# Decoder layer on one core: the output projection's second half with split attention operands, a 64 + 64 column tile for the sample rows, and gate-up low parts one slot ahead

## What is computed

```python
def mix_out(o_attn, conv_y, attn_out_g, conv_out_g, w_o):
    a = rmsnorm(o_attn.reshape(b, t, D_ATTN), attn_out_g)
    v = rmsnorm(conv_y, conv_out_g)
    return jnp.concatenate([a, v], axis=-1) @ w_o          # (576 x 1024) @ (1024 x 1024)
xp = xp + g1 * mix_out(...)                                # residual, per token set
h  = rmsnorm(xp, ln2_g) * (1 + sc2) + sh2
xp = xp + g2 * ((silu(h @ w_gate) * (h @ w_up)) @ w_down)  # w_gu: 1024 x 5632, w_down: 2816 x 1024
```

## Time and profile before

| | us |
|---|---|
| median of 3 runs | 933.33 |
| profiled execution | 940.86 |
| its span in the trace | 939.1 |
| TensorE busy | 910.1 (97%) |
| VectorE busy | 637.4 (68%) |
| ScalarE busy | 413.6 (44%) |
| GpSimd busy | 281.0 (30%) |

### The profile page before, as it was taken

How to read it: one execution, slowest core, us unless ns; L and a number is a source line. 1 busy time by engine, 2 the same in 40 slices (tenths; PEclk the granted TensorE clock), 3 DMA queues, 4 the chain that set the end, 5 groups by cost and what they waited for, 6 DMA issues and landing times.

```text
span 939.1 us, 16499 instructions
## 1 busy us (share of the span) xinstructions
PE 910.1 (97%) x6285; PEld 769.7 (82%) x6285; DVE 637.4 (68%) x1251; ACT 413.6 (44%) x823; POOL 281.0 (30%) x277
## 2 busy tenths in 40 slices
PE   6999999999999999999999998999999999999998
PEld 5777888899996666866775498999999999888886
DVE  3546585488837676768472799899889898443544
ACT  3655562142135343666840574444444446333221
POOL 4110100000015442444600217776777774000000
PEclk9989999999999999999999999999999999999999
DMA  8998603235248987196103163333333333522201
GB/s 266 386 362 272 199 27 114 90 119 222 89 139 309 335 322 266 57 303 173 36 1 112 68 180 85 96 90 91 91 95 103 108 101 109 194 90 90 73 0 51
DMA packets 84188, 138.83 MB, mean 148 GB/s; under 512 B 4180, under 2 KB 54948, under 8 KB 79759
## 3 DMA queue, kind: packets, MB, share of 16 engines
q1 hardware_dynamic: 74578, 96.26, 32.1%
q0 software_dynamic: 9248, 41.39, 12.5%
q10 hardware_dynamic: 284, 0.13, 0.1%
HBM read 130.58 MB, written 11.31 MB: 151 GB/s over the span
## 4 chain that ended last, share of the span: by engine, by line
PE 86%; DVE 6%; DMA 4%; ACT 2%; issue 2%; POOL 1%; SPq 0%; DVEq 0%; ACTq 0%
PE bank L2389 18%; PE bank L2391 18%; PE bank L2390 18%; PE bank L2383 9%; PE bank L2469 3%; PE bank L2910 3%; DMA wring<-in_w_ada 2%; PE bank L2750 2%; PE bank L2418 2%; PE bank L2720 2%; PE bank L2929 2%; PE bank L2883 2%; PE bank L2398 2%; PE bank L2399 2%; PE bank L2674 1%
## 5 line engine op out<-in xcount | busy, mean ns | idle before, releaser
L2389 PE MATMUL bank<-s,ring_hi 128*128 128x288 f32 x620 | 184.6, 298 | 2.7 <-DVE ring_lo L528 2.7
L2390 PE MATMUL bank<-s,ring_lo 128*128 128x288 f32 x620 | 183.6, 296 | 0.0
L2391 PE MATMUL bank<-s,ring_hi 128*128 128x288 f32 x620 | 183.0, 295 | 0.0
L2389 PEld LDWEIGHTS bank<-s,ring_hi 128*128 128x128 f32 x620 | 116.8, 188 | 3.2 <-DVE ring_lo L528 3.1
L2391 PEld LDWEIGHTS bank<-s,ring_hi 128*128 128x128 f32 x620 | 117.4, 189 | 0.0
L2390 PEld LDWEIGHTS bank<-s,ring_lo 128*128 128x128 f32 x620 | 117.1, 189 | 0.0
L528 DVE TENSOR_TENSOR ring_lo<-mem,ring_hi 128x512 fp32r<-128x512 f32 x84 | 108.3, 1325 | 0.8 <-POOL mem L980 0.5
L2383 PEld LDWEIGHTS bank<-cst,arena 128*128 128x128 f32 (+1 forms) x538 | 62.3, 148 | 21.0 <-issue 12.3
L2383 PE MATMUL bank<-cst,arena 128*128 128x128 f32 (+1 forms) x538 | 72.1, 288 | 7.5 <-DMA arena<-in_cache_k_cmp,idx 6.6
L528 DVE TENSOR_TENSOR dn_w<-wring,dn_w 128x2048 fp32r<-128x2048 f32 (+1 forms) x11 | 23.1, 2096 | 65.9 <-ACT dn_w L525 65.9
L900 POOL DMA_INDIRECT arena<-in_cache_k_slc,idh x16 | 15.4, 963 | 172.9 <-PE bank L2391 167.3
(11 more groups left out here) (385 smaller groups left out, 2112.9 us busy)
## 6 DMA issues: line engine op xcount, KB each, us to landing
wring<-in_w_gu SPq DMA_DIRECT2D x44, 512.0 KB, 5.3
wring<-in_w_ada SPq DMA_DIRECT2D x16, 1024.0 KB, 11.0
wring<-in_w_in SPq DMA_DIRECT2D x10, 1024.0 KB, 5.1
wring<-in_w_down SPq DMA_DIRECT2D x10, 1024.0 KB, 5.0
wring<-in_w_ada SPq DMA_DIRECT2D x16, 512.0 KB, 5.8
proj<-in_x_prompt SPq DMA_DIRECT2D x4, 512.0 KB, 11.9
mem<-in_state_k_win POOLq DMA_DIRECT2D x8, 256.0 KB
mem<-in_state_v_win POOLq DMA_DIRECT2D x8, 256.0 KB
```

What stands on the lines that cost most here:

```text
L2389: pe.matmul(dst, sh, ml, start=first and k == 0, stop=False)
L2390: pe.matmul(dst, sl, mh, start=False, stop=False)
L2391: ins = pe.matmul(dst, sh, mh, start=False, stop=last and k == len(pairs) - 1)
```

## The change

1. The heads of half n = 1 become split products, as in half n = 0. The third weight block (`wo`, 1, 0) gets high parts `last_hi` (four 512-column casts by ScalarE) and low parts `last_lo` (four subtractions by VectorE, in place of the raw block in the weight ring). `o_hi` and `o_lo` have to live through half n = 1, and move from `hbuf` to four places for the high part and onto `oT` itself for the low part; the casts and subtractions that made them in one instruction are now four, one for each slice.
2. The sample tile of half n = 0 (t = 4) goes through `products_tail`: the operands of convolution and heads carry 64 high and 64 low columns. ScalarE copies the lower half of the bank to `otmp`, VectorE adds it, and the gate multiplication follows as an instruction of its own.
3. One of the new places of `o_hi` is where the high part of operand m = 7, segment 0, lives later, so ScalarE makes that part later: it moves from behind m = 5 to behind `first_copy(1)`.
4. VectorE does `slot_rest(14)` ahead of its loop and `slot_rest(p + 8)` in each step, that in a step with m = 3 ahead of L2341 and L2344 as before.

```diff
-SEG_HIGH = [(0, 4), (0, 8), (0, 5), (0, 7), (0, 6), (1, 4), (1, 8), (2, 8), (2, 4), (1, 5), ...
+SEG_HIGH = [(0, 4), (0, 8), (0, 5), (0, 6), (1, 4), (1, 8), (2, 8), (2, 4), (0, 7), (1, 5), ...
...
+        o_hi = [pairs_at(f"o_hi{k}", z, c0, WIDE)[:, :] for k, (z, c0) in enumerate(((arows, 0), (arows, WIDE), (mem, 4 * TOK), (mem, 8192)))]
+        o_lo = pairs_at("o_lo", uvT, 0, 4 * TOK)[:, :].rearrange("p (k n) -> p k n", k=4)
+        last_hi = [pairs_at(f"wo_last{k}", z, c0, 512)[:, :] for k, (z, c0) in
+                   enumerate(((proj, 4608), (proj, 5120), (selb, 0), (mem, 8192 + WIDE)))]
...
ScalarE
+            def outputs_high(c0, c1):
+                for k in range(4):
+                    ins = high(act.copy, o_hi[k][:, c0:c1], oT[:, k, c0:c1])
+                ins.then_inc(o_high, 1)
...
-            high(act.copy, o_hi[:, :, 0:384], oT[:, :, 0:384]).then_inc(o_high, 1)
+            act.wait_ge(gates_out, 16)
+            outputs_high(0, 384)
...
-            high(act.copy, o_hi[:, :, 384:TOK], oT[:, :, 384:TOK]).then_inc(o_high, 1)
+            outputs_high(384, TOK)
+            weights(act, ("wo", 1, 0))
+            for k in range(4):
+                ins = high(act.copy, last_hi[k], last_raw[:, k])
+            ins.then_inc(wo_high, 1)
...
+            want_filled(act, ("wo", 0, 4))
+            act.copy(otmp[0:TS, :], ps(("wo", 0, 4))[TS:2 * TS, :]).then_inc(wo_tail, 1)
...
-                    for m in (5, 7, 6):
+                    for m in (5, 6):
                         sums_high(0, m)
...
             first_copy(1)
+            sums_high(0, 7)
...
VectorE
+            def outputs_low(c0, c1):
+                for k in range(4):
+                    if c1 == TOK:
+                        low(dve, o_hi[k][:, TOK:WIDE], oT[:, k, SEQ:TOK], o_hi[k][:, SEQ:TOK]).then_inc(dve_step, 1)
+                        steps[0] += 1
+                        dve.wait_ge(dve_step, steps[0])
+                    ins = low(dve, o_lo[:, k, c0:c1], oT[:, k, c0:c1], o_hi[k][:, c0:c1])
+                ins.then_inc(o_low, 1)
...
-            low(dve, c_lo, vT[:, :, 256:TOK], c_hi).then_inc(c_low, 1)
+            low(dve, c_lo, vT[:, :, 256:SEQ], c_hi[:, :, 0:256])
+            low(dve, c_hi[:, :, 320:384], vT[:, :, SEQ:TOK], c_hi[:, :, 256:320]).then_inc(c_low, 1)
...
+                        if not n and t == 4:
+                            dve.wait_ge(wo_tail, 1)
+                            frees(dve.tensor_tensor(x1t[0:P, :], ps(key)[0:P, :], otmp[0:P, :], ALU.add), key)
+                            want_emptied(dve, key)
+                            link(dve.tensor_tensor(x1t[0:P, :], x1t[0:P, :], gbc[0:P, t // 4, cols], ALU.mult))
...
+                    if not n and t == 2:
+                        dve.wait_ge(wo_high, 3)
+                        for k in range(4):
+                            ins = low(dve, last_lo[:, k], last_raw[:, k], last_hi[k])
+                        ins.then_inc(wo_low, 1)
...
             slot_rest(13)
+            slot_rest(14)
...
-                if p == 7 or FAST[p - 1][1] != 3:
-                    slot_rest(p + 7)
+                slot_rest(p + 8)
...
                 if m == 3:
-                    if p + 1 < NFAST:
-                        slot_rest(p + 8)
...
TensorE, project_conv
+                    if t == 4:
+                        products_tail(ps(key)[:, :], [(c_hi[:, kk, 256:384], (wo_hi[1][:, kk], wo_lo[1][:, kk])) for kk in range(4)],
+                                      True, False)
+                        return
...
TensorE, project_heads
+                pe.wait_ge(wo_low, 3 if n else 1)
+                pe.wait_ge(o_low, 1 + t // 3)
+                w = [(last_hi[k], last_lo[:, k]) if n else (wo_hi[0][:, k], wo_lo[0][:, k]) for k in range(4)]
+                if not n and t == 4:
+                    fills(products_tail(ps(key)[:, :], [(o_hi[k][:, SEQ:WIDE], w[k]) for k in range(4)], False, True), key)
                     return
-                wt = weights(pe, ("wo", n, 0))
-                for kk in range(4):
-                    last = pe.matmul(ps(key)[0:TM[t], :], oT[:, kk, 128 * t:128 * t + TM[t]], wt[:, kk, :], start=False, stop=kk == 3)
-                fills(last, key)
+                fills(products(ps(key)[0:TM[t], :], [((o_hi[k][:, c], o_lo[:, k, c]), w[k]) for k in range(4)], False, True), key)
```

More of the change, by code:

```diff
@@ L74 @@
 SEGS = ((2, 0, 96), (3, 96, 224), (4, 224, 288))
-SEG_HIGH = [(0, 4), (0, 8), (0, 5), (0, 7), (0, 6), (1, 4), (1, 8), (2, 8), (2, 4), (1, 5), (1, 7), (2, 5), (1, 6), (2, 7), (2, 6),
+SEG_HIGH = [(0, 4), (0, 8), (0, 5), (0, 6), (1, 4), (1, 8), (2, 8), (2, 4), (0, 7), (1, 5), (1, 7), (2, 5), (1, 6), (2, 7), (2, 6),
             (0, 3), (1, 3), (2, 3)]
@@ L432, in decoder_kernel @@
         wo_lo = [pairs_at(f"wo_lo{x}", wring, 2048 * r, 2048)[:, :].rearrange("p (k n) -> p k n", k=4) for x, r in enumerate(wo_at)]
-        c_hi, c_lo = (pairs_at(f"c_pair{y}", proj, 1280 * y, 1280)[:, :].rearrange("p (k n) -> p k n", k=4) for y in range(2))
-        o_hi, o_lo = (pairs_at(f"o_pair{y}", hbuf, 4 * TOK * y, 4 * TOK)[:, :].rearrange("p (k n) -> p k n", k=4) for y in range(2))
+        c_hi, c_lo = (pairs_at(f"c_pair{y}", proj, 1536 * y, 4 * n)[:, :].rearrange("p (k n) -> p k n", k=4) for y, n in enumerate((384, 256)))
+        o_hi = [pairs_at(f"o_hi{k}", z, c0, WIDE)[:, :] for k, (z, c0) in enumerate(((arows, 0), (arows, WIDE), (mem, 4 * TOK), (mem, 8192)))]
+        o_lo = pairs_at("o_lo", uvT, 0, 4 * TOK)[:, :].rearrange("p (k n) -> p k n", k=4)
+        last_hi = [pairs_at(f"wo_last{k}", z, c0, 512)[:, :] for k, (z, c0) in
+                   enumerate(((proj, 4608), (proj, 5120), (selb, 0), (mem, 8192 + WIDE)))]
+        last_raw = wch[:, chunk_of["wo", 1, 0] % WR]
+        last_lo = pairs_at("wo_last_lo", wring, 2048 * (chunk_of["wo", 1, 0] % WR), 2048)[:, :].rearrange("p (k n) -> p k n", k=4)
         g_rows = nc.dram_tensor("g_rows", [128, 512], F32).ap()
@@ L1322, in _ @@
             act.wait_ge(kvc_stored, 32)
-            high(act.copy, c_hi, vT[:, :, 256:TOK]).then_inc(c_high, 1)
+            high(act.copy, c_hi[:, :, 0:320], vT[:, :, 256:TOK]).then_inc(c_high, 1)
             weights(act, ("wo", 0, 1))
@@ L2095, in _ @@
             dve.wait_ge(o_high, 1)
-            low(dve, o_lo[:, :, 0:384], oT[:, :, 0:384], o_hi[:, :, 0:384]).then_inc(o_low, 1)
+            outputs_low(0, 384)
             key = ("oT", 4)
@@ L2112, in _ @@
             dve.wait_ge(o_high, 2)
-            low(dve, o_lo[:, :, 384:TOK], oT[:, :, 384:TOK], o_hi[:, :, 384:TOK]).then_inc(o_low, 1)
+            outputs_low(384, TOK)
             def second_norm(t):
@@ L2915, in project_heads @@
                 key = ("wo", n, t)
-                if n == 0:
-                    c = slice(128 * t, 128 * t + TM[t])
-                    pe.wait_ge(wo_low, 1)
-                    pe.wait_ge(o_low, 1 + t // 3)
-                    fills(products(ps(key)[0:TM[t], :], [((o_hi[:, kk, c], o_lo[:, kk, c]), (wo_hi[0][:, kk], wo_lo[0][:, kk]))
-                                                         for kk in range(4)], False, True), key)
-                    return
-                if t < 4:
-                    pe.wait_ge(o_ready, 1 + t // 3)
-                else:
-                    want_emptied(pe, ("oT", 4))
-                wt = weights(pe, ("wo", n, 0))
-                for kk in range(4):
-                    last = pe.matmul(ps(key)[0:TM[t], :], oT[:, kk, 128 * t:128 * t + TM[t]], wt[:, kk, :], start=False, stop=kk == 3)
-                fills(last, key)
+                c = slice(128 * t, 128 * t + TM[t])
+                pe.wait_ge(wo_low, 3 if n else 1)
[3 more added lines that the diff above has]
+                    fills(products_tail(ps(key)[:, :], [(o_hi[k][:, SEQ:WIDE], w[k]) for k in range(4)], False, True), key)
+                    return
+                fills(products(ps(key)[0:TM[t], :], [((o_hi[k][:, c], o_lo[:, k, c]), w[k]) for k in range(4)], False, True), key)
             def turn_sample():
```

10 lines of the change are left out of this document (5 added, 5 removed).

## The result

| | before | after |
|---|---|---|
| median (4 runs each) | 933.93 us (933.22 to 936.35) | 946.13 us (944.69 to 947.50) |
| ratio, 95% interval | | 1.0136 [1.0116, 1.0155] |
| profiled execution, its span | 940.86, 939.1 us | 945.81, 944.0 us |

A forecast was written before the change was run, and what follows sets the result against it. TensorE was taken to bound the kernel. The terms -1.9 (sample tile), -2.84 (heads) and +0.2 (order of low parts) sum to -4.5 us, so 928.8 us for the median, range 924.5 to 931.2.

The forecast's parts named there:

- What bounds the kernel: TensorE, busy 97% of the span; the output projection is bound by TensorE alone, with VectorE and ScalarE having time to spare.
- Parts 1 and 2: Output projection: split heads of half n = 1 give 2.84 us in tiles 0 to 3, 0.76 in tile 4; sample tile 1.9.
- The cover: Projection: low parts are ready before heads (0, 3), with 4.4 us to spare, and before (1, 0), so TensorE doesn't wait.
- What arrives: At the gate-up stage: 4.74 us of TensorE's 5.5 us arrive; 0.76 us becomes a wait at `turn_last`.
- The walk through the first tiles: Start of gate-up: VectorE and GpSimd turns followed to slot 19 in both orders; +0.2 us, bounds -1.2 and +1.2 us.
- the last sentence of part 4: Later gate-up stage: every slot has more than 1 us of margin in either order, so nothing is gained there.
- no wait from 600 on: Sign to look for: TensorE has no wait in the gate-up stage from 600 us on.
- The rival "slower": First tiles f: GpSimd takes each turn, VectorE loses 12 times 1.2 us over three tiles; 943 us, chance 0.03.
- The clock: Rival: behind slot 19's wait, now in pieces, the clock may not fall to 0.50; saves 1.7 us, 927.1 us, chance 0.22.

The follow-up runs named there:

- e1: Kernel after with VectorE's old order of slot low parts, projection edits kept; 929.74 us, ratio 0.9958 to before.
- e3: Kernel after with the low part of slot m = 3 moved behind the bank read L2355 in the m = 6 step; 930.13 us, ratio 0.9960 to before.
- e4: Kernel after with the low part in the m = 3 step moved behind the two gated products; 927.83 us, ratio 0.9944 to before.
- e6: The order of e3, with the two gated products of f = 1 moved to the end of step p = 12; 929.10 us, ratio 0.9956 to before.
- e10: e6 with the order of e4 for f > 1; 927.32 us, ratio 0.9939 to before.
- e9: Kernel after with a wait added: from f = 4 GpSimd makes slot m = 5 (L977) only behind the previous tile's gated products; 929.03 us, ratio 0.9957 to before.
- e8: Kernel after with TensorE doing product f = 8, m = 1 four more times, 6.4 us of additional work; 942.49 us, ratio 1.0089 to before.

## Why the prediction was wrong

The forecast was a gain of 4.5 us; it is a loss of 12.2 us. Point by point, in the order of its parts:

- **What bounds the kernel** was right for before. TensorE bound it, and it bounds e1, e3, e4, e6 and e10.
- **Parts 1 and 2 were right, but for 0.3 us.** The sample tile of half n = 0 gave 1.89 us where 1.9 was forecast. From the start of one tile of half n = 1 to the start of the next, tiles 0 to 2 gave 0.69 to 0.70 us each (0.71 was forecast), tile 3 gave 0.53, its distance holding the transposes of tile 2 (520.98, 0.09 us late, and 1.03 us long where they had taken 0.96), and tile 4 gave 0.68 (0.76 was forecast), its borders costing what was put at nothing. The cover held: no wait of TensorE at heads (0, 3) or (1, 0).
- **What arrives was right in its sum, its parts were a little off.** 4.79 us where 4.74 was forecast. TensorE came to the stage 5.19 us sooner (68.38 to 63.19) instead of 5.5, and 0.40 us of it went at `turn_last`, its wait being 0.34 and not 0.8 to 0.9. That the sum is right to 0.05 us is in part luck: two parts were off by 0.3 and by 0.4 us, and offset each other.
- **The walk through the first tiles was mis-sized.** The rows have 3.6 us of waits up to 600 us against 2.7, and by starts it is 4.9 against 3.2: 1.7 us more where the walk said +0.2, at most +1.2. It looked at slots 17 and 19 alone; there are five waits (565.52, 0.61 us, and 585.88, 588.31 among them).
- **The step that failed is the last sentence of part 4**, that later in the stage every slot has more than 1 us of margin in either order, and with it the sign "no wait from 600 on". The margins were read off the old order, slot by slot, against TensorE alone. But an in-order engine that waits 0.42 us for a cast delays what is queued behind it, here a bank read which GpSimd needs, behind which four GpSimd instructions stand, the last of which VectorE waits for. The prediction had asked this question of the waits that part 1 adds (what is queued behind it, and who waits for that) and not of the one that part 4 adds each tile. What the runs showed in its place is a ring of 12.25 us a tile against TensorE's 11.20, and sixteen waits, 16.6 us. The durations that the ring is made of, the 1.5 us of a lost turn among them, were to be had from the timelines of before; their chaining was not done.
- **The rival "slower" named half of the mechanism with the wrong reach.** The turns that the products lose are a needed link: with these gone the tile takes 11.36 us (e9). It gave them three tiles, and they last for 16; that its 943 us came near is luck, then. Its reason against, that the same instruction was back to 0.44 us from 587.54 on, described where the old order puts L972, not what the new order does to it; and it was read off L2341 alone, while the product behind it still lost its turn:

```profile
587.91 1.55 DVE L2344 TENSOR_TENSOR arena<-selb,uvT 128x288 f32<-128x288 f32 x1
```

  In before L972 starts at 653.18, 0.02 us behind the instruction that follows the two products (653.16), and it is 0.39 us behind L2344's start in every tile from 596.79 on. So they were neighbours in every tile, at a distance that a delay of the products by a few tenths eats up.
- **The other link**, the low part of slot m = 3 ahead of the read, was no rival at all. Cutting this link alone gives TensorE its 11.20 us a tile back (e3), as does taking the products out from behind the wait (e4); cutting the other leaves 0.16 us of the 1.04 (e9).
- **The clock.** It stayed at 1.00 through the gate-up stage of after: neither sixteen pauses of 0.80 us nor one of 1.65 us at 570.73 brought it down. The 1.7 us of that rival are in the result, then, buried under the loss. But its reason is not shown. In e1 the clock stayed at 1.00 behind a pause of 2.45 us, and in e3 it was at 0.50 (1.2 GHz, the lower of its two levels) for 3.4 us behind one of 2.01 us. The matmul behind the pause in e1, and in e3 with a window behind it:

```profile
569.34 0.40 PE L2430 MATMUL bank<-s,ring_hi 128*128 128x288 f32 x1 [2.45 <-DVE ring_lo L533]
...
571.55 0.61 PE L2429 MATMUL bank<-s,ring_hi 128*128 128x288 f32 x1 [2.01 <-DVE ring_lo L533]
571.60:574.90 3.30, 3.30 (x14) 3.30 (x15) 3.30 (x6) 0.83 (x2) 1.74 (x2) 0.50 0.69 199
```

  In e4 it fell as well, behind a pause of 2.73 us at 567.51. So the length of one pause doesn't decide it.

The Trainium skill's rule that I had weighed (SBUF — State Buffer, "SBUF: two separate sides": a VectorE instruction with two SBUF inputs and GpSimd hold the port pair in turn, whole instructions long) agrees with the traces again: L2383 took 1.57 us beside L980 at 671.77, and the same product took 0.45 us in e9 at 665.19, with GpSimd idle. The prediction took from it only that doing more subtractions swaps turns. What a turn cost here depended on which instruction lost it.

**What stays open.** When the clock falls behind a pause is open, as said. Why the first tiles have five waits in place of two was not followed row by row. Whether the ring could be shortened at GpSimd, with L985 ahead of L1004, was not tried.

## What to carry to other kernels

Moving work ahead on an in-order engine is only free if what it waits for is ready at the new place too: look for what it newly waits for, what is queued behind it, and follow that through the other engines until you are back. If you get back, sum the ring from start to start; the bound is the longest of the rings and the fullest engine, and busy shares show only the second (68% for VectorE in both kernels). A slack that was measured in one order says nothing about another, and two instructions that alternate at a port have a margin of their own, the distance between them.

## What the runs showed of the hardware

- VectorE's 128 x 288 product of two SBUF operands takes 0.45 us, and 1.53 to 1.58 us behind one GpSimd sum of 128 x 512. The same loss is harmless or costs 1 us a tile depending on which instruction bears it: from 600 us on before lost nothing by a mean of 1325 ns for the low parts of the slots made by GpSimd; after has 997 ns there and is slower.
- A kernel can be made faster with more work for its fullest engine (e8, 3.6 us for 6.4 us of it) or with a wait that is added (e9, 17.1 us).
- A matmul row with an idle time of 0.80 us stands for a loss of 1.07 us between starts. And at 11.36 us a tile (e9) TensorE shows no idle time at all in its rows; once a tile two distances between starts are 0.19 and 0.24 us in place of 0.13, and from 600 to 700 us there are 742 matmuls where e1 has 752.
- Going from float32 to float32r matmuls and back cost at most 0.02 us in a 128-row tile; in the 64-row tile the two halves took 0.14 us more than their own times.
